# Half of a gate's columns summed on VectorE, and attention heads that flow into the next jobs, in a one-core diffusion trunk kernel

## The chip, the cores and the metric

The kernel runs on one core of one Trainium2 chip. The metric is the device time of one execution in microseconds, the median of several runs. Below, PE is TensorE, DVE is VectorE, ACT is ScalarE, POOL is GpSimd and SP is SyncE, whose queue starts the weight transfers.

## What is computed

One layer (DEPTH = 1) of a diffusion trunk on 384 tokens: 128 context tokens (tile 0) and 256 latent tokens (tiles 1 and 2), in rows of 2048.

```
m = silu(cond) @ w_mod + b_mod       # two conditions: c_ctx and c
sh1, sc1, g1, sh2, sc2, g2 = split(m, 6)        # 2048 columns each
h = rms_norm(x, g_attn) * (1 + sc1) + sh1
z = h @ w_in        # heads A (6 q, 2 kv), B (6 q, 2 kv), C (4 q, low-rank kv)
o = concat(attention A (all keys), B (a band, with a sink logit), C (all keys))
x = x + g1 * (o @ w_o)
h = rms_norm(x, g_ffn) * (1 + sc2) + sh2
x = x + g2 * moe(h)                  # 32 experts of width 512, top 2 in the top group
```

All of it is float32. The change touches how m is computed for g1 and sh2 and at which moment, and where the last heads of the groups C and A are finished.

## The kernel before

**Steps.** A planner, `plan()`, writes one list of steps, and each engine walks this list in order and does its own part of every step. A job (`proj` or `kvc`) is one projection of one token tile into a PSUM bank: PE multiplies, ACT squares and copies the result to `zt`, POOL makes the reciprocal root, DVE scales it and applies the rotary turn (step `norm`), and two jobs later PE transposes it (step `turn`). In the jobs marked `attends` the `norm` step comes behind the heads placed after the job; in all others `job()` puts it in directly behind the job's projection and sums.

**Heads.** `advance(u)` appends, for a head-tile u: `qk` (PE scores, DVE maximum, ACT exponential), for an earlier one `pv` (PE values product, DVE copy of the output), `nz` (DVE normalises) and `pt` (PE transposes the probabilities, ACT copies them out). `advance()` without u only moves those on that have begun. Group C's twelve head-tiles stand behind aq1-0, aq1-1, aq1-2 and bq0-0, A's eighteen behind bq1 and bkv, and B's eighteen follow all jobs. Before the change C and A are each drained at their end by three `advance()`.

**Transposes.** `turn`, `cache` and `pt` share two PSUM banks in turn, numbered through. A C head's output is put into the last 128 columns of the bank that held its own probabilities. So `tp_bank` lets transpose number n wait until number n-2 has been read, and, if n-2 was a C head's `pt`, also until DVE has copied that head's output:

```
if n >= 2:
    pe.wait_ge(tp_read, n - 1)
if n - 2 in output_in:
    pe.wait_ge(o_ready, pv_units.index(output_in[n - 2]) + 1)
```

**Modulation.** sh1 and sc1 are done early. PE computes g1 and sc2 in "fillings": a step ("mod", g, k) takes one row of each partition out of a 1 MB unit, 8 matmuls of 512 columns in four column groups (`mod_step`), accumulated in `mod_ps`. The sixteen of g1 are spread over the drains and the heads of group A, the sixteen of sc2 lie between the heads of B. sh2 is summed by DVE (`shift_step`: four passes over 1024 columns for each of 16 units, 256 columns of each quarter in a half); after eight units `fold_low` adds the 128 partial rows up on PE into `mod_ps`. g2 is summed by DVE too, in the output projection (`g2_step`).

**Ring.** All weights pass through a ring of 12 slots of 1 MB. SP starts the transfers in the order of `units`, the one for unit m when unit m-12 has been used up. The four units of a projected chunk (such as in-bkv-0 to in-bkv-3) are used by three jobs, and come free one after another in the third.

Of the kernel before, what the change touches and what calls it, by code (L numbers as in the profile page):

```python
# [131 lines left out]
def const_layout():  # L132

    at, out = 0, {}
    for name, n in (("ident", P), ("pow", 4), ("fold", 3), ("ones", P), ("tri_b", P // 2), ("ones_b", P // 2), ("mask", 2 * P), ("cos", 2 * 64), ("sin", 2 * 64),
                    ("cosr", 2 * 32), ("sinr", 2 * 32), ("items", ITEMS), ("slots", P),
                    ("rev32", EXPERTS), ("rev4", GROUPS), ("experts", EXPERTS), ("tok", ASSIGN),
                    ("sel", 3), ("sel_low", 5),
                    ("caps", MAX_Q - 1)):
        out[name] = (at, n)  # L140
        at += n
    out["tokens"] = (at, T)
    return out, at


def constants():
# [41 lines left out]
    put("sel", np.array([[1.0, 0.0, 1.0]]))  # L188
    put("sel_low", np.array([[0.0, 0.0, 0.0, 1.0, 0.0]]))
    return c  # L190


def plan():
# [31 lines left out]
    for b, ks in ((2, (5, 6, 7, 8)), (3, (9, 10, 11, 12)), (4, (13, 14)), (5, (15,))):  # L225
# [3 lines left out]
        units.extend(("shift", n) for n in ks)  # L229
    later = [(g, k) for g in LATER_GROUPS for k in range(KD)]  # L230
    pending = []
    summed = [0]

    def job(kind, what, norm=True):
        jobs.append(what)
        if what == ("akv", 0):
            steps.append(("fold", 0))
        steps.append((kind, len(jobs) - 1))
        for _ in range(SUMMED[what[0]][what[1]] if what[0] in SUMMED else 0):
            units.append(("mod", SH2, summed[0]))  # L240
# [74 lines left out]
    for name, _, _ in CHUNKS:  # L315
# [27 lines left out]
    steps.append(("cache", "b"))  # L343
    steps.extend(("turn", n) for n in pending)
    assert summed[0] == KD and KD - 2 < len(later) <= KD
    attend("B", range(SHARE), fill=later[:SHARE * TILES])
# [43 lines left out]
def by_units(w_mod, b_mod, w_in, w_o, w2):  # L390

    out = {}
    for b, (at, w, n_units) in enumerate(BLOCKS):
        rows = w_mod[0].reshape(P, n_units, KD // n_units, 6, D)[..., at:at + w]
        out[f"w_scale{b}"] = rows[:, :, :, SC1].transpose(1, 0, 2, 3).reshape(n_units, P, D)
        if b == 0:
            out["w_shift0"] = rows[:, :, :, SH1].transpose(1, 0, 2, 3).reshape(n_units, P, D)
    rows = w_mod[0].reshape(P, KD // 2, 2, 6, 4, 2, 256)[:, :, :, SH2]
    out["w_low"] = rows.transpose(4, 1, 0, 2, 3, 5).reshape(KD, P, D)
    out["w_shift"] = w_mod[0][:, SH1 * D + SHIFT_FROM * P:(SH1 + 1) * D].T.reshape(KD - SHIFT_FROM, P, D)  # L400
# [11 lines left out]
def build(nc, ins, outs):  # L412
# [62 lines left out]
    with ExitStack() as ctx:  # L475
# [14 lines left out]
        csil = sb("csil", [P, KD, 3])  # L490
        csil_low = sb("csil_low", [P, 4])
        cvec = sb("cvec", [P, 2, KD])
# [253 lines left out]
        def unit_source(u, e=0):  # L746

            kind = u[0]
            if kind == "mod":
                _, g, k = u  # L750
                if g == SH2:
                    return ins["w_low"][k], (D,)
                return (ins["w_mod"][0].rearrange("(p j) n -> p j n", j=KD)[:, k, g * D:(g + 1) * D], (D,))
            if kind == "first":
                _, g, b, m = u
# [59 lines left out]
        for s in steps:  # L815
            if s[0] == "mod":
                m = unit_no[("mod", s[1], s[2])]
                if s[2] == KD - 1:
                    frees[m] = (mod_done, LATER_GROUPS.index(s[1]) + 2)
                    continue  # L820
                done = [m]
            elif s[0] in ("g2", "sum"):
                done = [unit_no[("mod", G2 if s[0] == "g2" else SH2, s[1])]]
            elif s[0] in ("proj", "kvc", "out"):
# [73 lines left out]
        def _(sp):  # L898
# [22 lines left out]
            for u in (17, *range(4), 11, *range(4, 8), 12, 8, 9, 10, 13, 14, 15, 18, 19, 16, 20, 21, 22, 23):  # L921
# [7 lines left out]
                else:  # L929
                    if u == EXTRA[1] - 1:  # L930
                        sp.wait_ge(mod_done, 2)
                    elif u == EXTRA[0]:
# [62 lines left out]
        def _(pe):  # L995
# [116 lines left out]
            def mod_step(g, k):  # L1112

                m = unit_no[("mod", g, k)]
                arrived(m)
                n = LATER_GROUPS.index(g)
                if k == 0:
                    pe.wait_ge(*((mod_read, n) if n else (z_ready, early[3] + 1)))
                low = (g, k) == (G1, 0)
                for q in range(4):  # L1120
                    mm = pe.matmul(mod_ps[32 * q:32 * q + (4 if low else 2), :], csil_low[:, :] if low else csil[:, k, 0:2], ring[:, ring_slot(m), q * 512:(q + 1) * 512],  # L1121
                                   start=(k == 0), stop=(k == KD - 1))
                mm.then_inc(*((slot_free[ring_slot(m)], 1) if k < KD - 1 else (mod_done, 1)))

            def fold_low(half):

                pe.wait_ge(*frees[unit_no[("mod", SH2, KD // 2 * half + KD // 2 - 1)]])
                for c in range(2):
                    for q in range(4):
                        mm = pe.matmul(mod_ps[32 * q:32 * q + 4, 256 * half:256 * half + 256], K("sel_low")[:, 1 - c:5 - c],  # L1130
                                       shift_sum[:, c, q * 256:(q + 1) * 256], start=False, stop=False)
                if half == 0:
                    mm.then_inc(mod_done, 1)
# [708 lines left out]
        def _(v):  # L1842
# [271 lines left out]
            def shift_step(k):  # L2114

                m = unit_no[("mod", SH2, k)]
                if k == 0:
                    after(v.memset(csil_low[:, :], 0.0))
                    v.tensor_copy(csil_low[:, 0:2], csil[:, 0, 0:2])
                elif k == KD // 2:  # L2120
                    v.wait_ge(mod_done, 1)
                if k:
                    v.wait_ge(*frees[unit_no[("mod", SH2, k - 1)]])
                v.wait_ge(*full_of(m))
                for i in range(2):
                    for c in range(2):
                        rows = ring[:, ring_slot(m), i * 1024:i * 1024 + 1024]
                        by = csil[:, 2 * (k % (KD // 2)) + i, c:c + 1]
                        if i:
                            v.wait_ge(v_step, own[0] - 1 + c)  # L2130
                        if i or k % (KD // 2):
                            last = v.scalar_tensor_tensor(out=shift_sum[:, c, :], in0=rows, scalar=by, in1=shift_sum[:, c, :],  # L2132
# [8 lines left out]
            for s in steps:  # L2141
                if s[0] == "g2":
                    g2_step(s[1])
                elif s[0] == "sum":
                    shift_step(s[1])
                elif s[0] == "mod" and s[2] == KD - 1:
                    g = s[1]
                    n = LATER_GROUPS.index(g)
                    v.wait_ge(mod_done, n + 2)
                    v.wait_ge(row_in, rows_in(n))  # L2150
# [97 lines left out]
                elif s[0] == "out":  # L2248
# [7 lines left out]
                    if n == FOLD_AT:  # L2256
                        v.wait_ge(mod_done, len(LATER_GROUPS) + 2)
                        v.tensor_copy(g2_sum[:, 0, 0:512], rank_ps[:, :]).then_inc(mod_read, 1)
# [201 lines left out]
        def _(g_):  # L2460
# [64 lines left out]
            for s in steps:  # L2525
                if s[0] == "mod" and s[2] == KD - 1:
                    store_row(s[1])
# [132 lines left out]
```

## Time and profile before

| | us |
|---|---|
| median of 3 runs | 1657.56 |
| lowest and highest | 1652.24, 1658.36 |
| the profiled execution, its own time | 1652.31 |
| span of its trace | 1650.2 |
| PE matmul busy | 1552.4 (94%) |
| DVE busy | 814.7 (49%) |

How to read it: all times of the trace are us from the start of the span. The jobs and heads that the change touches lie between 205 us and 516 us, the output projection follows until about 687 us, and behind that come the routing and the experts. The trace's rows tell which engine was busy, what an engine waited for, and when a transfer landed.

### The profile page before, as it was taken

Reading aid. Unit: us, or ns where it says so; the run is one execution under the profiler, and the core shown is the slowest. Engines: PE = TensorE matmul, PEld = TensorE weight load, DVE = VectorE, ACT = ScalarE, POOL = GpSimd, SP = SyncE. Lnnn points to the kernel's source line nnn. Section 1 sums busy time; section 2 is a strip of 40 time slices with the busy share of each in tenths; the row PEclk is TensorE's granted clock in tenths of the full one; section 3 lists DMA queues with packets and bytes.
Section 4 is the critical chain, followed back from the end, with each engine's and each line's share of the span. In section 5 each row is a group of like instructions: output and inputs, shape, how many; then the busy total and the mean of one; then the engine's idle time right before and its main releaser. Section 6 shows DMA issues by size and latency. Waiting matters only on the chain.

```text
span 1650.2 us, 18186 instructions
## 1 busy us (share of the span) xinstructions
PE 1552.4 (94%) x6534; PEld 648.0 (39%) x6579; DVE 814.7 (49%) x1473; ACT 282.6 (17%) x748; POOL 101.4 (6%) x185
## 2 busy tenths in 40 slices
PE   6999999999999999999989989988989998988998
PEld 3446655454434444543333233233233233323323
DVE  4774655762365972525525533543443442452544
ACT  3124231122231000111110110111011011011010
POOL 1013100000121001000000000000000000000000
PEclk9999999999999999999999999999999999999999
DMA  9993531567596783899999999999999999999997
GB/s 391 417 411 146 197 135 72 240 235 300 219 391 273 305 319 115 307 412 394 429 426 430 428 426 429 426 428 428 422 428 427 417 428 428 429 426 423 427 426 295
DMA packets 62126, 581.94 MB, mean 353 GB/s; under 512 B 9217, under 2 KB 10177, under 8 KB 16939
## 3 DMA queue, kind: packets, MB, share of 16 engines
q1 hardware_dynamic: 54848, 557.34, 81.7%
q0 software_dynamic: 5936, 23.23, 3.6%
q10 hardware_dynamic: 1296, 0.77, 0.2%
q8 instruction: 27, 0.44, 0.1%
q14 instruction: 19, 0.16, 0.0%
HBM read 584.07 MB, written 7.05 MB: 358 GB/s over the span
## 4 chain that ended last, share of the span: by engine, by line
PE 68%; DMA 16%; DVE 2%; issue 1%; ACT 1%; SPq 0%; POOL 0%; DVEq 0%; ACTq 0%; POOLq 0%
PE bank L1533 23%; DMA ring<-in_w 16%; PE bank L1263 11%; PE bank L1239 9%; PE bank L1436 7%; PE bank L1564 6%; PE bank L1354 2%; PE bank L1485 2%; PE bank L1121 1%; PE bank L1329 1%; PE bank L1583 1%; DVE r L2108 1%; PE bank L1508 1%; PE bank L1337 1%; PE bank L1546 1%
## 5 line engine op out<-in xcount | busy, mean ns | idle before, releaser
L1533 PE MATMUL bank<-ring,r 128*64 128x512 f32 x1920 | 445.5, 600 | 3.9 <-DMA ring<-in_w 3.9
L1564 PE MATMUL bank<-ring,mod_row 128*64 128x512 f32 x896 | 215.5, 637 | 49.9 <-DMA ring<-in_w 42.1
L1533 PEld LDWEIGHTS bank<-ring,r 128*64 128x64 f32 x1920 | 126.2, 136 | 255.8 <-issue 255.7
L1263 PE MATMUL bank<-ring,r 128*128 128x384 f32 (+2 forms) x672 | 225.5, 494 | 0.0
L2373 DVE TENSOR_TENSOR bank<-bank,r 128x512 f32<-128x512 f32 x180 | 125.3, 696 | 105.2 <-PE bank L1436 105.1
L1239 PE MATMUL bank<-ring,r 128*128 128x512 f32 x384 | 170.3, 595 | 1.5 <-issue 1.5
L1263 PEld LDWEIGHTS bank<-ring,r 128*128 128x128 f32 x672 | 123.6, 190 | 91.4 <-issue 43.7
L1564 PEld LDWEIGHTS bank<-ring,mod_row 128*64 128x64 f32 x896 | 78.2, 146 | 177.6 <-issue 167.4
L1436 PE MATMUL bank<-r 128*128 128x512 bf16 x495 | 132.2, 381 | 7.2 <-issue 7.2
L2375 DVE TENSOR_TENSOR r<-r,bank 128x512 f32<-128x512 f32 x180 | 123.7, 687 | 6.2
L2398 DVE TENSOR_SCALAR gains<-bank,w_now 128x512 f32<-128x512 f32 x30 | 22.5, 751 | 206.1 <-PE bank L1564 196.5
L1239 PEld LDWEIGHTS bank<-ring,r 128*128 128x128 f32 x384 | 71.0, 191 | 80.7 <-issue 80.6
L2381 DVE TENSOR_TENSOR gain_row<-gain_row,bank 128x512 f32<-128x512 f32 x16 | 11.0, 689 | 183.7 <-PE bank L1533 167.2
L1436 PEld LDWEIGHTS bank<-r 128*128 128x128 bf16 x540 | 40.6, 97 | 149.5 <-DVE r L2375 86.8
L1059 PE MATMUL bank<-r 128*128 128x512 f32 (+1 forms) x192 | 78.4, 557 | 1.3 <-DVE r L1895 1.1
L2108 DVE SCALAR_TENSOR_TENSOR r<-ring,csil,r 128x2048 f32<-128x2048 f32 x32 | 74.3, 2348 | 4.3 <-DMA r<-in_b_mod 3.8
L2132 DVE SCALAR_TENSOR_TENSOR spare<-ring,csil,spare 128x1024 f32<-128x1024 f32 x60 | 73.1, 1279 | 0.1
L1910 DVE CUSTOM_DVE_ANT_0 r<-ring,r 128x2048 bf16<-128x2048 f32 x28 | 65.8, 2351 | 9.4 <-ACT r L1630 7.4
L2222 DVE TENSOR_REDUCE small<-bank 128x1 f32<-128x384 f32 (+1 forms) x48 | 22.5, 468 | 82.6 <-PE bank L1329 58.8
L1792 ACT ACTIVATE gain_row<-bank 128x512 f32<-128x512 f32 x16 | 9.6, 597 | 308.9 <-PE bank L1533 295.2
L1786 ACT ACTIVATE r<-bank 128x512 f32<-128x512 f32 x30 | 17.8, 595 | 240.5 <-PE bank L1423 240.5
L2167 DVE SCALAR_TENSOR_TENSOR r<-r,small,gains 128x128 f32<-128x128 f32 (+2 forms) x91 | 27.5, 343 | 59.0 <-POOL small L2498 53.4
(306 smaller groups left out, 1279.4 us busy)
## 6 DMA issues: line engine op xcount, KB each, us to landing
ring<-in_w SPq DMA_DIRECT2D x174, 2048.0 KB, 17.8
ring<-in_w_mod SPq DMA_DIRECT2D x48, 1024.0 KB, 14.8
ring<-in_w SPq DMA_DIRECT2D x29, 1024.0 KB, 13.1
ring<-in_w_scale SPq DMA_DIRECT2D x16, 1024.0 KB, 23.5
ring<-in_w_shift SPq DMA_DIRECT2D x16, 1024.0 KB, 21.3
ring<-in_w_low SPq DMA_DIRECT2D x16, 1024.0 KB, 8.5
ring<-in_w_o SPq DMA_DIRECT2D x16, 1024.0 KB, 6.8
r<-mod_d POOLq DMA_DIRECT2D x8, 1024.0 KB, 7.5
```

The lines of the kernel that those rows point to most:

```text
L1059: mm = pe.matmul(early_bank[3 * c + t][:, 0:w], h_t[:, k, t * P:(t + 1) * P], early_w[c][i % 2][:, jj, :], start=(k == 0), stop=(k == KD - 1))
L1239: mm = pe.matmul(acc[acc_of(a)][:, :], qo[:, t, k, :], wu[:, j, :], start=(k == 0), stop=(k == KD - 1))
L1263: mm = pe.matmul(acc[acc_of(a)][:, 0:w], h_t[:, k, t * P:(t + 1) * P], wu[:, j, :], start=(k == 0), stop=(k == KD - 1))
L1354: mm = pe.matmul(out, v, prob_t[u % 2][:, i, :] if g == "C" else prob_ab[batch_of(u) % 2][:, i, :], start=(i == 0), stop=(i == len(tiles) ...
L1436: mm = pe.matmul(y_ps[k % 4][:, :], of_token[:, t * P:(t + 1) * P], y_part[:, n_part, c, :], start=(n_part == 0), stop=(n_part == 2))
L1533: mm = pe.matmul(ps[64 * c:64 * c + 64, :], xg_t[:, j, 64 * c:64 * c + 64], big_cut(slot_of(u), (8, 512))[:, j % 8, :], start=(j == 0), st ...
L1564: mm = pe.matmul(y_ps[c][64 * h:64 * h + 64, :], act_t[:, f, 64 * h:64 * h + 64], big_cut(slot_of(u), (2, D))[:, c % 2, f * 512:(f + 1) * ...
L1910: last = v.tensor_tensor_reduce(junk_s, w, cond_all[:, c, :], 1.0, b_shift[:, k:k + 1], ALU.mult, ALU.add, mod_t[:, 1, k, c:c + 1])
L2108: last = v.scalar_tensor_tensor(out=g2_sum[:, c, :], in0=ring[:, ring_slot(m), :], scalar=csil[:, k, c:c + 1], in1=g2_sum[:, c, :], op0=AL ...
L2132: last = v.scalar_tensor_tensor(out=shift_sum[:, c, :], in0=rows, scalar=by, in1=shift_sum[:, c, :], op0=ALU.mult, op1=ALU.add)
L2373: v.tensor_tensor(ps[:, :], ps[:, :], g2b[:, min(t, 1), cols], ALU.mult).then_inc(strip_scaled, 1)
L2375: return v.tensor_tensor(x1[:, t, cols], x1[:, t, cols], ps[:, :], ALU.add)
```

## The change

VectorE also sums the first 256 columns of each quarter of g1 (8 more units, 24 sums in all instead of 16, now steps ("sum", k)), in the jobs of bq0, bq1 and bkv. PE computes only the other half of g1, in 8 fillings instead of 16, each with 16 matmuls of 256 columns. There are three folds instead of two: before job bq0-2, before job bq1-1, and before g1's last filling; before the first one, four bf16 matmuls with zero weights open the accumulation in `mod_ps`. The drain of C is taken apart: its three `advance()` stand behind the jobs bq0-1, bq0-2 and akv-0. The drain of A is gone: its last head-tiles are moved on by the first of B. Of the fillings in C's drain (3), in bq1 (6) and in A's drain (2, one of g1 and one of sc2), two of bq1 remain; bkv keeps its six. The sums of g2 are split 2, 3, 3, 3, 3, 2 over the first six output jobs.

```diff
-SUMMED = {"aq0": (0, 1, 1), "aq1": (1, 1, 1), "bq0": (1, 1, 1), "akv": (2, 2, 2), "bq1": (1, 1, 0)}
-FOLD_LOW = 12
-G2_STEPS = (3, 3, 2, 3, 2, 3)
+HALVES = KD // 2
+LAST_MOD = {G1: HALVES - 1, SC2: KD - 1}
+SUMMED = {"aq0": (0, 1, 1), "aq1": (1, 1, 1), "bq0": (1, 2, 1), "akv": (2, 2, 2), "bq1": (1, 1, 1), "bkv": (2, 2, 2)}
+SUMS = 3 * HALVES
+FOLDS = {("bq0", 2): 0, ("bq1", 1): 1}
+G2_STEPS = (2, 3, 3, 3, 3, 2)
...
-        if (g, k) == (G1, FOLD_LOW):
-            steps.append(("fold", 1))
+        if (g, k) == (G1, LAST_MOD[G1]):
+            steps.append(("fold", 2))
         steps.append(("mod", g, k))
...
-        if what == ("akv", 0):
-            steps.append(("fold", 0))
+        if what in FOLDS:
+            steps.append(("fold", FOLDS[what]))
         steps.append((kind, len(jobs) - 1))
...
             job("proj", (name, t), norm=not attends)
             n = len(jobs) - 1
+            if (name, t) in (("bq0", 1), ("bq0", 2), ("akv", 0)):
+                advance()
...
             if (name, t) == ("bq0", 0):
-                attend("C", [TILES], flush=True, drain=(1, 1, 1))
+                attend("C", [TILES])
             if name == "bq1":
                 if t == 0:
                     steps.append(("turn", pending.pop(0)))
-                    attend("A", range(SHARE), [t], before=(1, 0, 1))
+                    attend("A", range(SHARE), [t], before=())
                 else:
-                    attend("A", range(SHARE), [t], before_pt=(0, 1), before_pv=(0, 0, 1))
+                    attend("A", range(SHARE), [t], before_pt=(0, 1))
...
-    for n in (1, 1, 0):
-        mods(n)
-        advance()
-    assert not scored and not turned_p
...
+                if g == G1:
+                    for i in range(2):
+                        for q in range(4):
+                            mm = pe.matmul(mod_ps[32 * q:32 * q + 2, 256:512], csil[:, 2 * k + i, 0:2],
+                                           ring[:, ring_slot(m), 1024 * i + 256 * q:1024 * i + 256 * q + 256],
+                                           start=False, stop=(k == LAST_MOD[G1] and i == 1))
...
+                first, at = (2, 256 * n) if n < 2 else (0, 0)
+                if n == 0:
+                    pe.wait_ge(z_ready, early[3] + 1)
+                    for q in range(4):
+                        pe.matmul(mod_ps[32 * q:32 * q + 4, :].rearrange("r (a n) -> r a n", a=4),
+                                  K("sel_low")[:, 4:6].bitcast(BF16), ones_b.unsqueeze(1).to_broadcast([P, 4, P]),
+                                  start=True, stop=False)
+                pe.wait_ge(*frees[unit_no[("sum", HALVES * n + HALVES - 1)]])
...
-                elif k == KD // 2:
-                    v.wait_ge(mod_done, 1)
+                if k and k % HALVES == 0:
+                    v.wait_ge(mod_done, k // HALVES)
```

## Rows read from the trace of the kernel before

**Rows 1.** Busy time by stretch: us, busy of each engine, granted clock, DMA share, GB/s

```profile
400.00:410.00 10.00, 10.00 (x35) 4.75 (x36) 2.21 (x9) 1.69 (x7) 0.40 (x1) 1.00 0.12 48
...
440.00:450.00 10.00, 7.93 (x51) 2.85 (x43) 6.03 (x21) 3.30 (x10) 1.23 (x3) 1.00 1.00 416
...
480.00:490.00 10.00, 9.58 (x48) 3.61 (x46) 6.70 (x24) 3.28 (x14) 0.00 (x0) 1.00 1.01 422
```

**Rows 2.** Chain that ended last, 262 to 294: start, us, line; a filling, a fold

```profile
265.24 0.97 PE bank L1121 x8
...
292.34 0.98 PE bank L1130 x16
```

**Rows 3.** Timeline of PE, job bq0-1: start, us, line, [idle before <- releaser]

```profile
270.88 10.49 PE L1263 MATMUL bank<-ring,r 128*128 128x384 f32 x32
```

**Rows 4.** Timelines of ACT, POOL and DVE, 258 to 352

```profile
292.05 0.28 ACT L1667 ACTIVATE r<-bank 128x128 f32<-128x128 f32 x1 [9.00 <-PE bank L1263]
...
293.69 0.85 POOL L2498 TENSOR_TENSOR small<-small,cst 128x3 f32<-128x3 f32 x1
...
268.92 0.29 DVE L2244 COPY r<-bank 128x128 f32<-128x128 f32 x1 [1.35 <-PE bank L1354]
...
272.07 4.87 DVE L2132 SCALAR_TENSOR_TENSOR spare<-ring,csil,spare 128x1024 f32<-128x1024 f32 x4
...
294.64 0.88 DVE L2167 SCALAR_TENSOR_TENSOR r<-r,small,gains 128x128 f32<-128x128 f32 x3 [3.13 <-POOL small L2498]
...
297.03 0.35 DVE L1967 TENSOR_TENSOR r<-r 128x192 f32<-128x192 f32 x1
```

**Rows 5.** Timeline of PE, group A's first heads, and of ACT beside them

```profile
348.13 0.68 PE L1329 MATMUL bank<-r 128*128 128x128 f32 x4 [0.59 <-ACT r L1741]
...
365.13 0.91 PE L1354 MATMUL bank<-r 128*128 128x384 f32 x2
...
364.25 0.27 ACT L1768 ACTIVATE r<-bank 128x128 f32<-128x128 f32 x1
```

**Rows 6.** DMA started between 427.6 and 428 us: KB, us to landing

```profile
ring<-in_w_mod SPq DMA_DIRECT2D x1, 1024.0 KB, 4.8
```

**Rows 7.** Timelines of PE and DVE, end of job bkv-2 and start of B

```profile
440.71 0.55 PE L1337 MATMUL bank<-cst,r 128*128 128x128 f32 x3
...
448.86 1.04 PE L1121 MATMUL bank<-ring,csil 128*2 128x512 f32 x8 [2.07 <-DVE mod_row L2151]
...
454.22 1.04 PE L1121 MATMUL bank<-ring,csil 128*2 128x512 f32 x8
...
438.87 0.56 DVE L2222 TENSOR_REDUCE small<-bank 128x1 f32<-128x384 f32 x1 [11.86 <-PE bank L1329]
...
447.83 0.28 DVE L1967 TENSOR_TENSOR r<-r 128x128 f32<-128x128 f32 x1
```

**Rows 8.** DMA started between 455.2 and 455.5 us, and PE's filling with it

```profile
ring<-in_w_mod SPq DMA_DIRECT2D x1, 1024.0 KB, 18.2
...
482.72 1.04 PE L1121 MATMUL bank<-ring,csil 128*2 128x512 f32 x8
```

**Rows 9.** Timeline of PE, end of B, around the first parts of the output projection

```profile
491.75 3.67 PE L1239 MATMUL bank<-ring,r 128*128 128x512 f32 x8 [1.50 <-issue]
...
503.16 2.20 PE L1354 MATMUL bank<-r 128*128 128x384 f32 x6 [1.71 <-ACT r L1768]
```

**Rows 10.** The page's group of g2's sums: count, busy us, mean ns

```profile
L2108 DVE SCALAR_TENSOR_TENSOR r<-ring,csil,r 128x2048 f32<-128x2048 f32 x32 | 74.3, 2348 | 4.3 <-DMA r<-in_b_mod 3.8
```

**Rows 11.** Timeline of PE at waits in the experts; busy time and clock behind one

```profile
844.09 7.09 PE L1564 MATMUL bank<-ring,mod_row 128*64 128x512 f32 x32 [0.56 <-DVE mod_row L2387]
854.81 10.09 PE L1564 MATMUL bank<-ring,mod_row 128*64 128x512 f32 x32 [3.63 <-DMA ring<-in_w]
...
1034.89 8.78 PE L1564 MATMUL bank<-ring,mod_row 128*64 128x512 f32 x32 [3.63 <-DMA ring<-in_w]
...
856.00:858.00 2.00, 2.00 (x6) 0.53 (x4) 0.00 (x0) 0.00 (x0) 0.00 (x0) 0.50 1.06 451
```

More of the change, by code:

```diff
@@ L137, in const_layout @@
                     ("rev32", EXPERTS), ("rev4", GROUPS), ("experts", EXPERTS), ("tok", ASSIGN),
-                    ("sel", 3), ("sel_low", 5),
+                    ("sel", 3), ("sel_low", 8),
                     ("caps", MAX_Q - 1)):
@@ L188, in constants @@
     put("sel", np.array([[1.0, 0.0, 1.0]]))
-    put("sel_low", np.array([[0.0, 0.0, 0.0, 1.0, 0.0]]))
+    put("sel_low", np.array([[0.0, 0.0, 0.0, 1.0, 0.0, 0.0, 0.0, 0.0]]))
     return c
@@ L229, in plan @@
         units.extend(("shift", n) for n in ks)
-    later = [(g, k) for g in LATER_GROUPS for k in range(KD)]
+    later = [(g, k) for g in LATER_GROUPS for k in range(LAST_MOD[g] + 1)]
     pending = []
@@ L235, in job @@
         jobs.append(what)
-        if what == ("akv", 0):
-            steps.append(("fold", 0))
+        if what in FOLDS:
+            steps.append(("fold", FOLDS[what]))
         steps.append((kind, len(jobs) - 1))
         for _ in range(SUMMED[what[0]][what[1]] if what[0] in SUMMED else 0):
-            units.append(("mod", SH2, summed[0]))
+            units.append(("sum", summed[0]))
             steps.append(("sum", summed[0]))
@@ L338, in plan @@
                 steps.append(("norm", n))
-    for n in (1, 1, 0):
-        mods(n)
-        advance()
-    assert not scored and not turned_p
     steps.append(("cache", "b"))
     steps.extend(("turn", n) for n in pending)
-    assert summed[0] == KD and KD - 2 < len(later) <= KD
+    assert summed[0] == SUMS and len(later) == KD
     attend("B", range(SHARE), fill=later[:SHARE * TILES])
@@ L397, in by_units @@
             out["w_shift0"] = rows[:, :, :, SH1].transpose(1, 0, 2, 3).reshape(n_units, P, D)
-    rows = w_mod[0].reshape(P, KD // 2, 2, 6, 4, 2, 256)[:, :, :, SH2]
-    out["w_low"] = rows.transpose(4, 1, 0, 2, 3, 5).reshape(KD, P, D)
+    rows = w_mod[0].reshape(P, HALVES, 2, 6, 4, 2, 256)[:, :, :, (SH2, G1)]
+    out["w_low"] = rows.transpose(3, 5, 1, 0, 2, 4, 6).reshape(4 * HALVES, P, D)
     out["w_shift"] = w_mod[0][:, SH1 * D + SHIFT_FROM * P:(SH1 + 1) * D].T.reshape(KD - SHIFT_FROM, P, D)
@@ L750, in unit_source @@
                 _, g, k = u
-                if g == SH2:
-                    return ins["w_low"][k], (D,)
+                if g == G1:
+                    return ins["w_low"][SUMS + k], (D,)
                 return (ins["w_mod"][0].rearrange("(p j) n -> p j n", j=KD)[:, k, g * D:(g + 1) * D], (D,))
+            if kind == "sum":
+                return ins["w_low"][u[1]], (D,)
             if kind == "first":
@@ L817, in build @@
                 m = unit_no[("mod", s[1], s[2])]
-                if s[2] == KD - 1:
-                    frees[m] = (mod_done, LATER_GROUPS.index(s[1]) + 2)
+                if s[2] == LAST_MOD[s[1]]:
+                    frees[m] = (mod_done, LATER_GROUPS.index(s[1]) + 3)
                     continue
@@ L822, in build @@
             elif s[0] in ("g2", "sum"):
-                done = [unit_no[("mod", G2 if s[0] == "g2" else SH2, s[1])]]
+                done = [unit_no[("mod", G2, s[1]) if s[0] == "g2" else s]]
             elif s[0] in ("proj", "kvc", "out"):
@@ L930, in _ @@
                     if u == EXTRA[1] - 1:
-                        sp.wait_ge(mod_done, 2)
+                        sp.wait_ge(mod_done, 3)
                     elif u == EXTRA[0]:
@@ L1115, in mod_step @@
                 arrived(m)
[L1116 to L1122, printed above, removed]
@@ L1123, in mod_step @@
-                mm.then_inc(*((slot_free[ring_slot(m)], 1) if k < KD - 1 else (mod_done, 1)))
-            def fold_low(half):
-                pe.wait_ge(*frees[unit_no[("mod", SH2, KD // 2 * half + KD // 2 - 1)]])
+                if g == G1:
+                    for i in range(2):
[3 more added lines that the diff above has]
+                                           start=False, stop=(k == LAST_MOD[G1] and i == 1))
+                else:
+                    if k == 0:
+                        pe.wait_ge(mod_read, LATER_GROUPS.index(g))
+                    for q in range(4):
+                        mm = pe.matmul(mod_ps[32 * q:32 * q + 2, :], csil[:, k, 0:2], ring[:, ring_slot(m), q * 512:(q + 1) * 512],
+                                       start=(k == 0), stop=(k == KD - 1))
@@ new lines, in mod_step, with fold_low @@
+                mm.then_inc(*((slot_free[ring_slot(m)], 1) if k < LAST_MOD[g] else (mod_done, 1)))
+            def fold_low(n):
+                first, at = (2, 256 * n) if n < 2 else (0, 0)
+                if n == 0:
+                    pe.wait_ge(z_ready, early[3] + 1)
+                    for q in range(4):
+                        pe.matmul(mod_ps[32 * q:32 * q + 4, :].rearrange("r (a n) -> r a n", a=4),
+                                  K("sel_low")[:, 4:6].bitcast(BF16), ones_b.unsqueeze(1).to_broadcast([P, 4, P]),
+                                  start=True, stop=False)
+                pe.wait_ge(*frees[unit_no[("sum", HALVES * n + HALVES - 1)]])
@@ L1128, in fold_low @@
                 for c in range(2):
+                    row = first + c
                     for q in range(4):
-                        mm = pe.matmul(mod_ps[32 * q:32 * q + 4, 256 * half:256 * half + 256], K("sel_low")[:, 1 - c:5 - c],
+                        mm = pe.matmul(mod_ps[32 * q:32 * q + 4, at:at + 256], K("sel_low")[:, 3 - row:7 - row],
                                        shift_sum[:, c, q * 256:(q + 1) * 256], start=False, stop=False)
-                if half == 0:
+                if n < 2:
@@ L2114, in shift_step @@
             def shift_step(k):
[L2116 to L2119, printed above, removed]
-                elif k == KD // 2:
-                    v.wait_ge(mod_done, 1)
+                m = unit_no[("sum", k)]
+                if k and k % HALVES == 0:
+                    v.wait_ge(mod_done, k // HALVES)
                 if k:
-                    v.wait_ge(*frees[unit_no[("mod", SH2, k - 1)]])
+                    v.wait_ge(*frees[unit_no[("sum", k - 1)]])
                 v.wait_ge(*full_of(m))
@@ L2145, in _ @@
                     shift_step(s[1])
-                elif s[0] == "mod" and s[2] == KD - 1:
+                elif s[0] == "mod" and s[2] == LAST_MOD[s[1]]:
                     g = s[1]
                     n = LATER_GROUPS.index(g)
-                    v.wait_ge(mod_done, n + 2)
+                    v.wait_ge(mod_done, n + 3)
                     v.wait_ge(row_in, rows_in(n))
@@ L2256, in _ @@
                     if n == FOLD_AT:
-                        v.wait_ge(mod_done, len(LATER_GROUPS) + 2)
+                        v.wait_ge(mod_done, len(LATER_GROUPS) + 3)
                         v.tensor_copy(g2_sum[:, 0, 0:512], rank_ps[:, :]).then_inc(mod_read, 1)
@@ L2525, in _ @@
             for s in steps:
-                if s[0] == "mod" and s[2] == KD - 1:
+                if s[0] == "mod" and s[2] == LAST_MOD[s[1]]:
                     store_row(s[1])
```

5 lines of the change are left out of this document (2 added, 3 removed).

## The prediction, on record before the changed kernel ran

> **What bounds the kernel now.** I read the busy times by stretch first. In the stage of the change PE is the bound: between 400 and 410 us it is busy 10.00 of 10.00 us while DMA has a share of 0.12. In B's heads two things are near their limit at once, PE at 9.58 and DMA at 1.01 with 422 GB/s [rows 1]. So a filling taken off PE is worth its PE time, unless PE was waiting there anyway, and in B what comes late through the ring counts too. The chain that ended last gives the prices: 0.97 us for a filling, 0.98 us for a fold of 16 matmuls of 256 columns [rows 2]. The new filling has the same 16 matmuls of 256 columns, so I price it at 0.98 us. The timelines of the single engines then show who waits for whom. The output projection behind is PE's work without gaps, and the experts' transfers wait for slots that it frees, so I let what is lost or won until 516 us pass to the end in full.
>
> **The drain of C.** Before, PE goes through three fillings and the last `pv` and `pt` of C to job bq0-1 at 270.88, and the timeline shows no gap of PE there [rows 3]. After it, these `pv` and `pt` stand behind the jobs bq0-1, bq0-2 and akv-0. I followed the numbers of the transposes there: pt9, turn aq1-2, pt10, turn bq0-0, pt11, turn bq0-1, cache-a. Each of pt10, pt11 and cache-a is two behind a C head's `pt`, so `tp_bank` makes PE wait for DVE's copy of the output of head-tile 9, 10 and 11. These three jobs are not marked `attends`: in DVE's order the job's `norm` stands ahead of that copy. So PE, with its next projection queued behind the transpose, waits for the whole chain of the job that it has just finished.
>
> The chain's length is read off job bq0-2 before: ACT begins at 292.05, POOL ends at 294.54, DVE scales from 294.64 and ends the rotary turn at 297.38; the copy takes 0.29 [rows 4]. That is 5.6 us from ACT's begin, and PE gets to its next instruction some 0.2 us sooner (my estimate), so 5.8. Of this PE fills the first job's with a turn and a one-tile `pv` (some 0.3 each, estimates), the second's with a turn and a three-tile `pv` (0.91 [rows 5]). For akv-0 the chain has no rotary turn (1.86 us less, from 295.52 to 297.38), so 4.0 us, of which 1.2 are filled. The waits are 5.2 + 4.6 + 2.8 = 12.6 us. Three fillings are gone (-2.9), and the zero matmuls cost some 0.2. Sum: +9.9 us. Bounds of the waits: 0, if DVE had copied in time after all, and 12.6; I know no row that says less than the chain. The added sums do not lengthen it: two take 9.8 us at 4.87 each [rows 4] against 10.5 us of projection [rows 3], and end before POOL is done.
>
> **Group A.** In bq1-0 two fillings go. PE waited 0.59 us for ACT although one stood in front of it [rows 5], and the other covers the first exponentials; I value both at 0 (bound -1.9). In bq1-1 and bq1-2 one each goes, in front of a `pv` that needs ACT's copy of the transpose; that copy ended at 364.52 and the `pv` began at 365.13, so each brings 0.6 rather than 0.97: -1.2 us together [rows 5]. The second fold only moves.
>
> **Job bkv-2.** Here DVE sums two units more, and they come late. Counting 12 units back, the slots of sums 22 and 23 are those of in-bkv-0 and in-bkv-1, and these come free only in job bkv-2 itself. Before, the first of these slots was given its next transfer at 427.7, with 4.8 us to landing [rows 6]. So the sums run from 432.5 to 442.3, while DVE's first maximum behind them began at 438.87; with the small operations behind it (some 1.2 us in all, an estimate) that left 0.6 us to spare until PE's transpose at 440.71 [rows 7]. Late next is that transpose, by 2.8 us (bounds 0 and 5). The third fold adds 0.98. Sum: +3.8 us.
>
> **From A to B.** The drain goes, with PE's 2.07 us wait for DVE to read `mod_ps` [rows 7]. What stays is the turn of bkv-2 behind DVE's norm, which ended at 448.1; sc2's first filling could start at 448.5. Until the point that was at 454.22 it leaves 3.7 us of work (filling 0.97, two `pt` of some 0.33, an estimate, one `pv` of 2.1 as in [rows 9]), so 452.2: -2.0 us.
>
> **The end of B.** One more filling among the heads moves sc2's last one and the parts of the output projection each one head further. The 1.50 us before the first part, where the profile names no releaser, is by the code's wait DVE's copy of an output behind the two additions for sc2; the 1.71 us is a `pv` directly behind its transpose [rows 9]. After the change a head, and a part of 3.4 us, lie between: -3.2 us (bounds -3.2 and 0).
>
> **Transfers in B.** Four of the slots that come free in bkv-2 held sc2's units before; now they take sums 22 and 23 and g1's last two fillings, so that sc2 and w_o come five units later, 5 x 2.5 = 12.4 us at 422 GB/s [rows 1]. The unit of sc2's filling 13 landed at 473.5 (18.2 us after its start) and was used at 482.72, 9.2 us later [rows 8]; its use moves about 2.6 us back. It lands 0.6 us late, others a little more. I take +1.0 us (bounds 0 and 6).
>
> **g2's sums.** A unit costs 2 x 2.35 us [rows 10], three cost 14.1 against four parts of some 3.5 us and the transposes between them [rows 9]. DVE starts with two instead of three and stays within the reserve of half a job that the transposes leave it: 0.
>
> Sum: 9.9 - 1.2 + 3.8 - 2.0 - 3.2 + 1.0 = +8.3 us.
>
> **The clock.** Behind a wait of 3.63 us for DMA the granted clock stood at 0.50, the 1.2 GHz level, and 32 matmuls took 10.09 us where the same group took 7.09 at 2.4 GHz, and 8.78 behind another such wait [rows 11]; the 2.07 us at 448.86 left the granted clock at 1.00 [rows 1, 7]. The first two new waits are longer than 3.63 us, so I add 1.7 for each, the lower of the two prices: +3.4 us (bounds 0 and 9). The trace agrees with the rule of the Trainium skill, in "TensorE: Matmul & The Clock Gate", section "Part 1: The HAM clock gate", that the default state is the throttled one and that activity releases it. By that rule the change would cost the 11.7 us of this sum, without it 8.3.
>
> Sum with the clock: +11.7 us. The profiled execution took 1652.31 us (span 1650.2), so it would take 1664.0; against the median of 1657.56 I predict 1669.3 us.
>
> **Rivals.** (1) The waits are there but cost less: the clock holds, and the late sums or transfers are hidden. For it speaks that PE kept its clock at 448.86; against it the length of the waits. 8.3 less 2.8 and 1.0 gives +4.5 us, 1662. (2) No wait at the C transposes, which ends on the other side: if DVE had the copies ready and every cover held, PE's own work decides: -2.9 + 0.2 - 1.9 + 1.0 - 2.0 - 3.2 = -8.8 us, 1648.8. It decides from the point at which DVE copies before the transpose is due, so its `norm` would have to end within 1 us of the projection instead of 5.5; the code's order speaks against that. (3) B becomes bound by transfers: five units late in full cost up to 6 us on top, 1675; the lead of 9.2 us before speaks against more.
>
> **Chances.** The forecast (waits at all three C transposes, the net beyond +8.3) 0.64; rival 1 0.20; rival 3 on top 0.08; rival 2, whole or in part, 0.08. A measurement of this kernel tells about 0.5%, 8.3 us, from no change. Faster by more than that: 0.05, within: 0.26, slower: 0.69. The range is 1657 to 1677: below it lies most of rival 2, above it the clock at its upper bound with rival 3.
>
> **What the profile after would show.** PE idle for about 5, 4.6 and 2.8 us ahead of the transposes behind bq0-1, bq0-2 and akv-0, released by DVE's copy, and a granted clock of 0.5 behind the first two; job akv-1 about 10 us later than before. In bkv-2, PE idle about 3 us ahead of a transpose, with DVE in its sums. No wait ahead of sc2's first filling or of the first output part. If PE doesn't wait behind bq0-1, the prediction is wrong and rival 2 stands; if it waits but the clock stays at 1.00, the time is near 1666.

## The result, and the profile after

The changed kernel takes 1668.0 us (median of 5 runs, 1667.31 to 1669.77), the kernel before 1656.31 us in the same comparison (5 runs, 1652.24 to 1658.36). The ratio is 1.0074, with a 95% interval of 1.0063 to 1.0085: slower by 0.7%, and +11.7 us of medians. The two profiled spans lie further apart, 1665.4 against 1650.2 us: the profiled execution of before (1652.31, mean granted clock 0.987) is near the low end of its runs, the one of after (1667.6, clock 0.982) near the middle. Places and durations below are from the traces, the price of a whole version is from the medians.

The view of waits comes first: what PE waited for between 200 and 530 us in the kernel after the change (engine, line <- releaser: us in total, times, longest).

```profile
PE bank L1352 <- issue: 9.8, 2, 5.1
PE bank L1352 <- DVE r L2249: 3.2, 3, 2.8
PE bank L1325 <- issue: 2.8, 1, 2.8
```

L1352 is the transpose of a `pt` step, L1325 that of a `cache` step. For the first and third group the profile names only "issue", that is, no releaser; in the code the wait there is `tp_bank`'s, for a count of heads copied. The timelines of the kernel after show what ended just before PE went on (columns as in [rows 3]). PE:

```profile
265.17 10.49 PE L1278 MATMUL bank<-ring,r 128*128 128x384 f32 x32
...
275.82 0.39 PE L1369 MATMUL bank<-r 128*128 128x128 f32 x2
281.31 0.87 PE L1352 MATMUL bank<-cst,r 128*128 128x128 f32 x3 [5.11 <-issue]
...
282.49 1.93 PE L1145 MATMUL bank<-spare,cst 128*4 128x256 f32 x16
284.35 11.39 PE L1278 MATMUL bank<-ring,r 128*128 128x384 f32 x32
...
301.40 0.88 PE L1352 MATMUL bank<-cst,r 128*128 128x128 f32 x3 [4.66 <-issue]
302.07 16.10 PE L1278 MATMUL bank<-ring,r 128*128 128x512 f32 x32
...
321.93 0.41 PE L1325 MATMUL bank<-cst,r 128*128 128x128 f32 x2 [2.77 <-issue]
```

and DVE beside the first wait:

```profile
278.27 0.88 DVE L2179 SCALAR_TENSOR_TENSOR r<-r,small,gains 128x128 f32<-128x128 f32 x3 [1.72 <-POOL small L2510]
...
280.66 0.35 DVE L1982 TENSOR_TENSOR r<-r 128x192 f32<-128x192 f32 x1
280.92 0.28 DVE L2256 COPY r<-bank 128x128 f32<-128x128 f32 x1
```

PE had nothing left to do at 276.2; the copy of the head's output ended at 281.20, directly behind the rotary turn, and PE went on at 281.31. The reader is to see also what comes behind: the fold took 1.86 us from its start to the next instruction (284.35 less 282.49), where the chain of before has 0.98 for one [rows 2]; the projection of 384 columns took 11.39 against 10.49 [rows 3], and the one of 512 columns 16.10 us, where the next two such jobs took 13.90 each. Busy time by stretch of the kernel after, from the same places (the stretch and its length, then busy time and count of PE, PE's weight load, DVE, ACT and POOL, then the granted clock, DMA share and GB/s):

```profile
281.00:283.00 2.00, 1.69 (x15) 0.84 (x19) 0.70 (x4) 0.49 (x1) 0.00 (x0) 0.50 0.00 0
...
302.00:304.00 2.00, 2.00 (x5) 0.97 (x4) 2.00 (x3) 0.49 (x1) 0.00 (x0) 0.50 0.98 414
...
365.00:367.00 2.00, 2.00 (x17) 0.41 (x17) 1.35 (x7) 0.62 (x3) 0.00 (x0) 0.50 1.01 426
...
461.00:463.00 2.00, 2.00 (x26) 0.59 (x17) 0.00 (x0) 0.00 (x0) 0.00 (x0) 0.50 1.02 429
```

These are four stretches at the 1.2 GHz level; the trace of before has none between 50 us and the experts. The third lies behind job bq1-0, where the fillings had gone, the fourth behind the late sums of bkv-2. DVE's timeline in bkv-2 shows the sum that came late:

```profile
447.84 9.78 DVE L2144 SCALAR_TENSOR_TENSOR spare<-ring,csil,spare 128x1024 f32<-128x1024 f32 x8 [5.49 <-DMA ring<-in_w_low]
457.54 0.55 DVE L2234 TENSOR_REDUCE small<-bank 128x1 f32<-128x384 f32 x1
```

PE's timeline of the same kernel, from bq1-0, from bkv-2 to B, and at the end of B:

```profile
362.67 0.68 PE L1344 MATMUL bank<-r 128*128 128x128 f32 x4 [1.55 <-ACT r L1756]
364.19 0.53 PE L1344 MATMUL bank<-r 128*128 128x128 f32 x2 [0.84 <-ACT r L1768]
...
365.19 1.89 PE L1145 MATMUL bank<-spare,cst 128*4 128x256 f32 x16
...
458.95 0.52 PE L1352 MATMUL bank<-cst,r 128*128 128x128 f32 x3 [2.82 <-DVE r L2249]
...
467.30 0.44 PE L1319 MATMUL bank<-cst,r 128*128 128x128 f32 x2 [0.98 <-ACT r L1783]
469.02 0.41 PE L1319 MATMUL bank<-cst,r 128*128 128x128 f32 x2 [1.28 <-DVE r L1982]
469.36 1.04 PE L1128 MATMUL bank<-ring,csil 128*2 128x512 f32 x8
...
510.06 3.60 PE L1254 MATMUL bank<-ring,r 128*128 128x512 f32 x8
...
531.21 2.11 PE L1195 MATMUL bank<-gains,mod_t 128*1 128x36 f32 x64
```

The answers to [rows 7] and [rows 9] are here: no wait ahead of sc2's first filling (469.36), none ahead of the first part of the output projection (510.06). The last row, PE's row product for the shift, is a good mark for the end of the stage. In the trace of before it begins at 515.93, here at 531.21: +15.28 us. The spans differ by 15.2, so what was lost in this stage passed to the end in full.

### The profile page after: what moved, and what is told of

Its sections match the earlier page's. It is cut to its first block, busy times and chain, and to the rows that moved or that the text cites. A ratio compares the mean times of both kernels' runs of the same rounds, so it can differ in the third digit from the quotient of the medians.

```text
span 1665.4 us, 18308 instructions
## 1 busy us (share of the span) xinstructions
PE 1560.7 (94%) x6599; PEld 652.3 (39%) x6599; DVE 852.1 (51%) x1503; ACT 282.3 (17%) x748; POOL 102.4 (6%) x185
## 4 chain that ended last, share of the span: by engine, by line
PE 63%; DMA 17%; DVE 6%; issue 2%; ACT 1%; SPq 0%; POOL 0%; ACTq 0%; DVEq 0%; POOLq 0%
PE bank L1548 22%; DMA ring<-in_w 16%; PE bank L1278 11%; PE bank L1451 7%; PE bank L1579 6%; PE bank L1254 5%; DVE r L2123 4%; PE bank L1500 2%; PE bank L1369 2%; PE bank L1344 1%; PE bank L1598 1%; PE bank L1523 1%; PE bank L1352 1%; PE bank L1561 1%; PE bank L1232 1%
## 5 line engine op out<-in xcount | busy, mean ns | idle before, releaser
L1278 PE MATMUL bank<-ring,r 128*128 128x384 f32 (+2 forms) x672 | 229.0, 499 | 0.0
L1451 PE MATMUL bank<-r 128*128 128x512 bf16 x540 | 142.4, 382 | 0.0
L2144 DVE SCALAR_TENSOR_TENSOR spare<-ring,csil,spare 128x1024 f32<-128x1024 f32 x90 | 109.7, 1279 | 5.7 <-DMA ring<-in_w_low 5.5
L1682 ACT ACTIVATE r<-bank 128x128 f32<-128x128 f32 (+1 forms) x76 | 20.9, 284 | 214.6 <-PE bank L1278 208.8
```

Source lines behind the costliest of these rows:

```text
L1278: mm = pe.matmul(acc[acc_of(a)][:, 0:w], h_t[:, k, t * P:(t + 1) * P], wu[:, j, :], start=(k == 0), stop=(k == KD - 1))
L1451: mm = pe.matmul(y_ps[k % 4][:, :], of_token[:, t * P:(t + 1) * P], y_part[:, n_part, c, :], start=(n_part == 0), stop=(n_part == 2))
```

## The experiments

The comparison runs give the kernel before 1655.99 us with the first four, 1655.45 with the next three and 1656.3 with the last two. Each edit is against the changed kernel unless another is named. Line numbers in a run's rows are those of its own kernel.

**1. norm behind the head step.** It changes only the order in which DVE does two things.

```diff
-            job("proj", (name, t), norm=not attends)
+            late = (name, t) in (("bq0", 1), ("bq0", 2), ("akv", 0))
+            job("proj", (name, t), norm=not attends and not late)
             n = len(jobs) - 1
-            if (name, t) in (("bq0", 1), ("bq0", 2), ("akv", 0)):
+            if late:
                 advance()
+                steps.append(("norm", n))
```

> The changed kernel, but in the jobs bq0-1, bq0-2 and akv-0 the step norm stands behind the head-tile step, so that VectorE copies the output before it waits for the job's own reciprocal root. Theory (the copy queued behind norm holds the transpose): the three waits of 5.1, 4.7 and 2.8 us shrink to under 1 us each and the two stretches at the lower clock behind the first two go, some 4 us; 1652 us (1650 to 1655). Rival 1 (the waits without any price of the clock): 1656. Rival 2 (the transposes wait for something else, such as ScalarE's read of the bank): the waits stay, 1667 to 1669.

Measured: 1651.98 us, ratio 0.9975 (0.9962 to 0.9988), faster than the kernel before. PE's timeline of its trace, at the three steps:

```profile
277.40 0.52 PE L1354 MATMUL bank<-cst,r 128*128 128x128 f32 x3 [0.65 <-issue]
...
279.04 10.59 PE L1280 MATMUL bank<-ring,r 128*128 128x384 f32 x32
...
291.05 0.52 PE L1354 MATMUL bank<-cst,r 128*128 128x128 f32 x3 [0.43 <-issue]
291.40 13.90 PE L1280 MATMUL bank<-ring,r 128*128 128x512 f32 x32
...
306.73 0.41 PE L1327 MATMUL bank<-cst,r 128*128 128x128 f32 x2 [0.43 <-issue]
```

The waits are 0.65, 0.43 and 0.43 us, and the projections are back at 10.59 and 13.90. The copy queued behind `norm` was the cause, worth 16.0 us of medians with the clock; rivals 1 and 2 of this run fall. The traces put nearly all of it where the edit is: from the start of job bq0-1 to that of akv-1 the changed kernel takes 57.01 us (322.18 less 265.17), this one 41.25 (306.97 less 265.72).

**2. The waits kept, PE busy in them.** Matmuls whose result nobody reads are put in front of the three waiting steps.

```diff
+            def warm(s):
+                n = {("pt", 10): 7, ("pt", 11): 6, ("cache", "a"): 3}.get(s, 0)
+                if n:
+                    pe.wait_ge(e_ready, 12)
+                for _ in range(n):
+                    pe.matmul(sc_ps[0][:, 0:T], h_t[:, 0, 0:P], h_t[:, 0, :], start=True, stop=True)
+
             def tp_bank(s):
+                warm(s)
```

> The changed kernel with matmuls that nobody reads, put in front of the three waiting steps (7, 6 and 3 of 128x384, some 4.5, 3.9 and 1.9 us of a score bank that is free then), so that the waits end when they did but TensorE is busy in them. Theory (behind the long waits the lower clock costs some 4 us): granted clock 1.00 through that stretch, 1664 us (1662 to 1665.5). Rival (the clock costs nothing there, all of it is the waits): 1667 to 1669. If the added matmuls outlast the waits, more than 1669.

Measured: 1663.96 us, ratio 1.0050 (1.0036 to 1.0064). PE's transpose begins when it did (281.26, in the changed kernel 281.31), but the clock stays. PE's timeline of this run:

```profile
275.99 4.68 PE L1158 MATMUL bank<-r 128*128 128x384 f32 x14
281.26 0.52 PE L1360 MATMUL bank<-cst,r 128*128 128x128 f32 x3 [0.59 <-issue]
...
281.93 1.03 PE L1145 MATMUL bank<-spare,cst 128*4 128x256 f32 x16
```

The busy time by stretch (the granted clock is the third number from the end of a row):

```profile
280.00:290.00 10.00, 9.40 (x48) 5.04 (x47) 5.42 (x11) 0.49 (x1) 0.00 (x0) 1.00 0.30 108
...
300.00:310.00 10.00, 10.00 (x25) 4.49 (x24) 8.70 (x8) 0.19 (x1) 0.00 (x0) 1.00 0.64 268
```

So the clock behind the two long waits costs 4.0 us of medians (1668.0 less 1663.96; 3.9 of spans, 1665.4 less 1661.5), and the waits themselves the other 12 of the 16. The traces, from bq0-1 to akv-1, divide it much the same way: 57.01 us in the changed kernel, 52.31 here, 41.25 in run 1, so 4.7 for the clock and 11.06 for the waits, which were 12.54 us and of which run 1 keeps 1.51.

**3. Two sums one job sooner**, out of bkv-2 into bq1.

```diff
-SUMMED = {... "bq1": (1, 1, 1), "bkv": (2, 2, 2)}
+SUMMED = {... "bq1": (1, 2, 2), "bkv": (2, 2, 0)}
```

> The changed kernel with the last sums one job earlier: (1, 2, 2) in bq1 and (2, 2, 0) in bkv in place of (1, 1, 1) and (2, 2, 2). Theory (sums 22 and 23 were late because their slots come free in bkv-2 only): the 2.8 us wait in bkv-2 and the lower clock behind it go, 1663.5 us (1662 to 1665.5). Rival (VectorE has no room for 24 sums anywhere in these jobs): the wait moves into bq1, 1667 to 1669.

Measured: 1667.39 us, ratio 1.0064 (1.0039 to 1.0089), on four runs. That is 0.6 us under the changed kernel, inside the scatter of either: by time the theory missed, and the time is the one that the rival gave. The trace bears out a part of each. The 2.82 us of bkv-2 are gone, as the theory says, but a wait of 1.21 us is new in bq1-2, as the rival says, where two sums and the `norm` of the job before are too much for a job of 10.5 us. PE's timeline of this run:

```profile
398.33 0.52 PE L1352 MATMUL bank<-cst,r 128*128 128x128 f32 x3 [1.21 <-DVE r L2249]
...
469.57 1.83 PE L1128 MATMUL bank<-ring,csil 128*2 128x512 f32 x8
```

The other row shows a filling of 1.83 us behind the waits at the turns, where the changed kernel took 1.04 (at 469.36): the lower clock, at another place. In this execution PE had also begun bq0-1 at 267.07, 1.9 us late, with a mean granted clock of 0.97 between 200 and 265 us, ahead of all that the edit touches. From there to the mark it took 263.4 us (530.50 less 267.07) against 266.0 of the changed kernel. Of the 2.6 us, 0.8 lie before akv-1 (56.19 against 57.01 us), where the edit changes nothing; how much of the other 1.8 the median would show is open.

**4. The sums without the spread.** Both drains are whole again, without fillings.

```diff
-            if (name, t) in (("bq0", 1), ("bq0", 2), ("akv", 0)):
-                advance()
...
-                attend("C", [TILES])
+                attend("C", [TILES], flush=True)
...
+    for _ in range(3):
+        advance()
     steps.append(("cache", "b"))
```

> The sums without the other part: the changed kernel with both drains whole again, at bq0-0 and behind bkv-2, with no fillings in them. Theory (the spread of C's drain is what makes it slower): the waits of 12.5 us and their clock go, bare drains cost 1 to 3 us each, 1655 us (1652.5 to 1658). Rival (the sums themselves cost more than they bring): above 1660.

Measured: 1657.23 us, ratio 1.0010 (0.9997 to 1.0022): like the kernel before. What eight fillings less could give back is spent in the bare drains: C's takes as long as it did with three fillings (job bq0-1 begins at 270.87, before the change at 270.88), with waits of 0.99, 0.58 and 0.58 us for ACT in their place. At the end of A there were, on the same line, 2.92, 0.94 and 2.00 us of waiting for DVE, and a `pv` at the lower clock took 4.21 us instead of 2.20. PE's timeline of this run:

```profile
453.90 0.66 PE L1352 MATMUL bank<-cst,r 128*128 128x128 f32 x3 [2.00 <-DVE r L2249]
455.14 4.21 PE L1369 MATMUL bank<-r 128*128 128x384 f32 x6 [0.58 <-ACT r L1783]
```

**5. Both kinds of wait mended:** the edit of run 1, and one sum moved, not two: `"bq1": (1, 2, 1), "bkv": (2, 2, 1)`.

> The changed kernel with norm behind the head-tile step in bq0-1, bq0-2 and akv-0, and one sum moved from bkv-2 to bq1-1: (1, 2, 1) in bq1 and (2, 2, 1) in bkv, so that bkv-2 has one late unit and not two. Theory (both kinds of wait are mended): none of the waits of 5.1, 4.7, 2.8 and 2.8 us is left above 1 us, 3 to 4.5 us less than with norm behind alone (1652.0), 1648 us (1646.5 to 1650). Rival (a sum less in bkv-2 is paid for by a wait in bq1, as when two were moved): 1651 to 1653.

Measured: 1649.67 us, ratio 0.9961 (0.9948 to 0.9974), 2.3 us under run 1, less than expected but in the range. No wait for DVE is left in bkv-2 or bq1-2. A new one is there, in B and for the ring, in PE's timeline of this run:

```profile
469.13 1.04 PE L1130 MATMUL bank<-ring,csil 128*2 128x512 f32 x8 [2.27 <-DMA ring<-in_w_mod]
```

**6. The fillings where PE waits anyway:** on top of 5, the two of bq1 in its first job.

```diff
-                    attend("A", range(SHARE), [t], before=())
+                    attend("A", range(SHARE), [t], before=(1, 0, 1))
...
-                    attend("A", range(SHARE), [t], before_pt=(0, 1))
+                    attend("A", range(SHARE), [t])
```

> The kernel of both_mended, with the two fillings of bq1 among the heads of bq1-0 (before the first and the third) in place of one each in bq1-1 and bq1-2. Theory (bq1-0 waits 1.6 and 0.8 us for ScalarE without fillings, so that they are free there, while in the other two each costs 0.6 us): 1.2 us less than both_mended. Rival (no difference): the waits in bq1-1 and bq1-2 grow by what the fillings covered.

Measured: 1648.46 us, ratio 0.9963 (0.9950 to 0.9975). The medians are 1.2 us apart, as expected, but the intervals overlap almost wholly and the ratio is no lower than run 5's, so by time no gain is shown. The traces show half of it. The wait of 1.55 us in bq1-0 is 0.59 again, and from the start of bq1-0 to the fold behind it PE takes 14.85 us with the two fillings (349.74 less 334.89) and took 14.84 without them (349.12 less 334.28): they are free there. Job bkv-0 begins 117.2 us behind bq0-1 (382.79 less 265.61) against 117.8 (382.84 less 265.00), 0.7 us less and not 1.2: where the fillings had been in bq1-1 and bq1-2, waits of 0.56 and 0.48 us for DVE are new, as the rival had it.

**7. The spread without the sums,** against the kernel before:

```diff
             n = len(jobs) - 1
+            if (name, t) in (("bq0", 1), ("bq0", 2), ("akv", 0)):
+                mods(1)
+                advance()
...
-                attend("C", [TILES], flush=True, drain=(1, 1, 1))
+                attend("C", [TILES])
```

> The other part alone: the kernel before, all its fillings and sums kept, with C's drain spread over bq0-1, bq0-2 and akv-0, one of its three fillings ahead of each. Theory (the spread makes the waits, with or without the sums): PE waits 4.2, 3.7 and 1.8 us there, the fillings being hidden in them, and loses 3 to 4 us by the clock; 1656 + 9.7 + 3.5 = 1669 us (1666 to 1671). Rival (the waits come from the added sums in VectorE's order): under 1660.

Measured: 1670.67 us, ratio 1.0091 (1.0075 to 1.0108). The waits are 3.95, 3.50 and 2.77 us, the last where 1.8 was expected. PE's timeline of this run:

```profile
281.18 0.88 PE L1340 MATMUL bank<-cst,r 128*128 128x128 f32 x3 [3.95 <-issue]
281.85 12.63 PE L1266 MATMUL bank<-ring,r 128*128 128x384 f32 x32
...
321.90 0.41 PE L1313 MATMUL bank<-cst,r 128*128 128x128 f32 x2 [2.77 <-issue]
```

For akv-0 the filling hides nothing. ACT's timeline has its copy of the new values begin only behind the last C `pv`:

```profile
319.17 0.38 ACT L1677 ACTIVATE r<-bank 128x256 f32<-128x256 f32 x1 [1.53 <-PE bank L1357]
```

The filling stands in front of that `pv`, and so it only moves the chain back. With 15 us for the spread alone and 1.2 for the sums alone (run 4), the sums are not what makes the kernel slower.

**8. B's end one head sooner,** on top of run 6: sc2's first filling stands between the turns of bkv-1 and bkv-2.

```diff
     steps.append(("cache", "b"))
-    steps.extend(("turn", n) for n in pending)
...
+    steps.append(("turn", pending[0]))
+    mods(1)
+    steps.append(("turn", pending[1]))
```

> The kernel of fillings_first, with sc2's first filling between the turns of bkv-1 and bkv-2, so that all sc2 fillings and the first two parts of the output projection stand one head sooner, as before the change. Theory (the 1.50 and 1.71 us at B's end came from that place): both waits are back, and the filling hides 1 of the 1.3 us in front of the turn of bkv-2; 2.2 us more than fillings_first, 1650.7 us. Rival (these waits had gone for another reason, such as the changed load of VectorE): no wait there, 1 us less.

Measured: 1652.95 us, ratio 0.9974 (0.9965 to 0.9983). That is 4.5 us over run 6 where 2.2 were expected; but the kernel before took 0.85 us more in this comparison too, and the two intervals overlap, so the size is not settled by time. The trace settles the mechanism: both waits of [rows 9] are back to the hundredth. Waits for the ring are there too, which the expectation did not have. PE's timeline of this run:

```profile
460.50 1.04 PE L1132 MATMUL bank<-ring,csil 128*2 128x512 f32 x8 [2.07 <-DMA ring<-in_w_mod]
...
468.45 1.04 PE L1132 MATMUL bank<-ring,csil 128*2 128x512 f32 x8 [2.42 <-DMA ring<-in_w_mod]
...
492.57 3.67 PE L1258 MATMUL bank<-ring,r 128*128 128x512 f32 x8 [1.50 <-issue]
503.98 2.20 PE L1373 MATMUL bank<-r 128*128 128x384 f32 x6 [1.71 <-ACT r L1787]
```

**9. The same with no filling at B's first head** (`later.insert(0, None)`, an empty place in the list of fillings), so that all behind it stands as in run 6.

> As one_head_sooner, but with no filling at B's first head, so that from the second head on all stands where it did in fillings_first. Theory: the filling hides 1 of the 1.3 us in front of the turn of bkv-2, no wait at B's end, 1 us less than fillings_first, 1647.5 us, unless transfers in B, which kept a filling waiting 0.4 us there, take it back. Rival: no difference, since B's heads are held by the ring: 1648.5 us.

Measured: 1649.71 us, ratio 0.9958 (0.9941 to 0.9975). The wait in front of the turn of bkv-2 fell from 1.27 to 0.32 us and B's end stayed free, but PE waited 0.38 and 2.40 us for the ring in B. The medians do not tell it from run 6. The forecast gain is not there; by the trace it was the waits for the ring that took it back, as the expectation had allowed for, and that is read from one execution.

## Why the prediction came true

Forecast: 1669.3 us, +11.7 over the median. Measured: 1668.0, +11.7 over the median of its comparison. The mechanism was right, the agreement to the tenth is luck. The terms of the forecast were worked out from the trace of before, and against the trace of after they add up to too little: +15.28 us at the mark, not +11.7. Up to akv-1, 13.3 us were forecast (9.9 and the clock's 3.4) and 14.55 found (322.18 less 307.63, although the sign given for it was "about 10 us", without the clock); from there to job bkv-2, -1.2 forecast and +0.79 found (439.41 less 424.07 makes 15.34); from there to the mark, -0.4 forecast and -0.06 found. The medians lie 11.7 us apart all the same, since the profiled execution of before lies 4.0 us under the median of its comparison and the one of after 0.4.

- **The drain of C.** Waits of 5.2, 4.6 and 2.8 us were forecast; 5.11, 4.66 and 2.77 were found. Run 1 shows the cause (DVE's order), run 7 that it needs no added sum. One row was misread at no cost: the 0.91 us for the three-tile `pv` is one of group A; C's took 0.83 in the trace of after.
- **The clock.** The mechanism held, the size was too small. Forecast were 3.4 us behind the first two waits; run 2 measures 4.0 us of medians and 4.7 by the traces. Not forecast were the stretches behind bq1-0 and bkv-2. In the trace they turn the fold before bq1-1 into 1.89 us, the projection behind it into 11.03, and third fold and last g1 filling into 1.89 and 1.93: about 1.4 and 1.6 us more than the same work took at 2.4 GHz, counted from start to start, argued from these durations and not tested by a run. They are the largest part of what the forecast lacked.
- **Group A.** The value of 0 for the fillings of bq1-0 is right for the time of its heads: 14.85 us with them in run 6, 14.84 without in run 5. Without them PE stood still for 1.55 and 0.84 us instead of 0.59, and in the changed kernel the clock fell there. That the missing fillings alone did it isn't shown: runs 1, 4 and 5 have the same two waits, and the fold behind them took 1.05 us, at the 2.4 GHz level. In bq1-1 and bq1-2, PE now waits 0.34 and 0.55 us in front of the `pv`: the removed fillings brought 0.6 and 0.4 us of their 0.97, against 0.6 each forecast.
- **Job bkv-2.** 2.8 us were forecast, 2.82 found, with DVE waiting 5.49 us for its unit; the sum begins 8.4 us behind the job's start (447.84 less 439.41), as the forecast had it (432.5 less 424.07). Run 5, with one late unit less, has no wait there.
- **From A to B.** The wait of 2.07 us for `mod_ps` is gone; 0.98 and 1.28 us at the last two turns are in its place. The second is the one that the step expected, for bkv-2's `norm`; the first, for ACT, it did not name.
- **The end of B.** Both waits, 1.50 and 1.71 us, are gone, and run 8 brings them back by place alone. For the first the profile names no releaser. The forecast took it from the code to be DVE's copy behind the two additions for sc2, and DVE's timeline of the kernel before agrees: the copy ended at 491.65, PE went on at 491.75 [rows 9].

```profile
488.53 0.68 DVE L2151 TENSOR_TENSOR mod_row<-bank,mod_row 128x512 f32<-128x512 f32 x1
489.25 0.69 DVE L2154 SCALAR_TENSOR_TENSOR mod_row<-mod_row,gain_row 128x512 f32<-128x512 f32 x1
...
491.10 0.55 DVE L2246 COPY r<-bank 128x384 f32<-128x384 f32 x1
```

- **Transfers in B.** The one term that missed the other way: +1.0 forecast, no wait found. Of the stalls it seems to be the one of bkv-2 that gave the ring time. Run 1, 16 us faster but with that stall kept, begins sc2's first filling 30.0 us behind job bkv-2's start (452.81 less 422.78), as the changed kernel does (469.36 less 439.41), and doesn't wait for the ring either; run 5, without it, begins it 25.4 us behind (447.48 less 422.07) and waits 2.27 us, run 9 2.40. So the forecast saw the shortage, but put it into a kernel where the stall of bkv-2, which it had forecast too, covered it. That is argued from one trace of each, and run 5 also has its sums queued in another order: run 3, without the stall too and with both late sums queued earlier, shows no wait for the ring.
- **g2's sums** cost nothing, as forecast: from the mark at 531.21 on, the kernel takes the time of before.

Rival 2, that no C transpose waits, gave 1648.8 us for the change, 8.8 under the median of before. The mended kernels of runs 5 and 6 are 5.8 and 7.0 us under it (1649.67 and 1648.46 against 1655.45): most of the gain aimed at was there, and the three waits at C's transposes and the one of bkv-2 stood in front of it.

## What to carry to other kernels

When a step is moved past another in a shared list, read the order of every engine, not of the one that is to gain: here PE's transpose waited for a DVE copy, DVE did the new job's normalisation first, and that needed a projection that PE had only just finished. A buffer of two in turn makes such a wait with no name: write out the numbers of its users around the moved step and see who is two behind. Work that is spread into other jobs should go where the engine waits anyway (by the traces of runs 5 and 6, two fillings cost nothing in bq1-0), and units of a ring that depend on slots of the same job come late however early they are queued (bkv-2).

## What the runs showed of the hardware

The granted clock did not follow the length of a single wait. It fell to 0.50 behind waits of 5.11 and 4.66 us, and also behind 1.55 and 0.84 us close together in bq1-0, and 2.82 in bkv-2; it stayed at 1.00 behind the 2.77 us at akv-0, as busy time by stretch of the kernel after shows:

```profile
318.00:322.00 4.00, 1.23 (x11) 1.06 (x10) 0.98 (x4) 1.67 (x7) 1.97 (x4) 1.00 0.00 0
322.00:324.00 2.00, 2.00 (x7) 1.04 (x8) 2.00 (x2) 0.38 (x1) 0.08 (x1) 1.00 0.50 139
```

Nor is the same pair of waits always followed by a fall. PE's timeline of run 1 has them in bq1-0 too, and the fold behind them took 1.05 us, at the 2.4 GHz level, where it took 1.89 in the changed kernel:

```profile
347.47 0.68 PE L1346 MATMUL bank<-r 128*128 128x128 f32 x4 [1.56 <-ACT r L1758]
348.99 0.49 PE L1346 MATMUL bank<-r 128*128 128x128 f32 x2 [0.84 <-ACT r L1770]
349.84 1.05 PE L1147 MATMUL bank<-spare,cst 128*4 128x256 f32 x16
```

So stalls of 1 to 2 us among small matmuls can cost more than their own length (here some 1.4 us more), but do not always, and the place of a fall differs from one version to the next. Executions of one and the same kernel differ in it as well: of the 24 of the kernel before that were taken beside the first four runs, the three fastest (1652.61 to 1654.06 us) have a mean granted clock of 0.987 and the four slowest (1658.61 to 1660.69) of 0.981 or 0.982. It is one reason why medians of this kernel do not settle differences of 1 to 2 us.
